# A two-block transformer layer on one core: the gate matrix made by adding scatter DMAs, and a reordered scan stage

## The reference

```python
def _gla_chunked(q, k, v, logf, s0):            # 8 heads, chunks of 64, two directions
    bc = cumsum(logf, axis=3)
    scores = where(incl, (q * exp(bc - ref)) @ (k * exp(ref - bc)).T, 0)
    o_intra = scores @ v
    def step(S, xs):
        o_c = (q * exp(bc)) @ S
        S = tot_c[..., :, None] * S + (k * exp(bc[-1] - bc)).T @ v
        return S, o_c
...
def _peer(h, w_query, sub_keys, expert_u, expert_v):
    q = (t @ w_query).reshape(n_tok, 8, 2, 128)
    sc = einsum('thcd,hckd->thck', q, sub_keys)
    s1, i1 = top_k(sc[:, :, 0], 16); s2, i2 = top_k(sc[:, :, 1], 16)
    top_s, top_i = top_k(s1[..., :, None] + s2[..., None, :], 16)
    e1, e2 = i1[top_i // 16], i2[top_i % 16]
    experts, gates = e1 * 128 + e2, softmax(top_s)
    act = gelu(einsum('td,tkd->tk', t, expert_u[experts])) * gates
    y = einsum('tk,tkd->td', act, expert_v[experts])
```

## Time and profile before

| | us |
|---|---|
| median of the runs | 5435.87 |
| the profiled execution | 5440.96 |
| its span, first to last instruction | 5439.2 |
| TensorE busy | 4832.4 (89%) |
| VectorE busy | 3114.6 (57%) |
| ScalarE busy | 2083.3 (38%) |
| POOL busy | 65.8 (1%) |
| scan stage | 3223 to 3549 |
| peer stage | 3769 to 5439 |

### The profile page before, as it was taken

The page is one execution under the profiler, slowest core; times in us unless marked ns, Lnnn a source line. Parts: engine busy times, 40 slices in busy tenths (PEclk is TensorE's granted clock), DMA queues, the critical chain, the costliest instruction groups (busy, mean ns, idle before and its releaser), DMA issues. The chain is left out here.

```text
span 5439.2 us, 67843 instructions
## 1 busy us (share of the span) xinstructions
PE 4832.4 (89%) x24244; PEld 3935.6 (72%) x24244; DVE 3114.6 (57%) x5040; ACT 2083.3 (38%) x2398; POOL 65.8 (1%) x137
## 2 busy tenths in 40 slices
PE   8926799999999569999799975677999999899998
PEld 3923477877877458878699965533888888788887
DVE  0062388888888642233688856512887666344444
ACT  1000267767767301111455545411333444322222
POOL 1000100000000100000000000000000000000000
PEclk9557899999999779999799986688999999999999
DMA  8412599999999623244111011142333454666663
GB/s 345 147 39 91 203 355 367 371 364 367 369 365 368 248 112 109 106 137 141 55 34 36 28 40 47 37 157 102 124 127 127 173 200 170 221 196 191 197 192 120
DMA packets 256059, 976.23 MB, mean 179 GB/s; under 512 B 27060, under 2 KB 63492, under 8 KB 202212
## 3 DMA queue, kind: packets, MB, share of 16 engines
q1 hardware_dynamic: 248516, 923.74, 47.5%
q0 software_dynamic: 7392, 50.50, 2.3%
HBM read 799.87 MB, written 174.28 MB: 179 GB/s over the span
## 5 line engine op out<-in xcount | busy, mean ns | idle before, releaser
L84 PE MATMUL peer_bank<-peer_t_high,peer_high 128*128 128x512 f32 x2176 | 856.4, 394 | 49.4 <-DVE peer_low L2771 35.8
L86 PE MATMUL peer_bank<-peer_t_high,peer_low 128*128 128x512 f32 x2176 | 849.9, 391 | 0.0
L85 PE MATMUL peer_bank<-peer_t_low,peer_high 128*128 128x512 f32 x2176 | 848.2, 390 | 0.0
L2771 DVE TENSOR_TENSOR peer_low<-peer_raw,peer_high 128x1024 fp32r<-128x1024 f32 x272 | 332.6, 1224 | 622.0 <-ACT peer_high L3112 622.0
L1076 DVE TENSOR_TENSOR moe_low<-moe_raw,moe_high 128x2048 fp32r<-128x2048 f32 x256 | 574.6, 2286 | 55.9 <-ACT moe_high L984 53.0
L84 PEld LDWEIGHTS peer_bank<-peer_t_high,peer_high 128*128 128x128 f32 x2176 | 409.9, 188 | 133.1 <-issue 50.6
L984 ACT ACTIVATE moe_high<-moe_raw 128x2048 fp32r<-128x2048 f32 x256 | 478.3, 1906 | 3.7 <-PE moe_up_bank L894 2.0
L3112 ACT ACTIVATE peer_high<-peer_raw 128x1024 fp32r<-128x1024 f32 x272 | 287.0, 1056 | 486.2 <-PE peer_bank L86 481.0
L86 PEld LDWEIGHTS peer_bank<-peer_t_high,peer_low 128*128 128x128 f32 x2176 | 409.5, 188 | 87.0
L85 PEld LDWEIGHTS peer_bank<-peer_t_low,peer_high 128*128 128x128 f32 x2176 | 410.0, 188 | 83.5
L1081 DVE TENSOR_TENSOR moe_low<-moe_raw,moe_high 128x2048 fp32r<-128x2048 f32 x128 | 293.0, 2289 | 66.4 <-ACT moe_high L989 66.4
(11 more groups left out here) (535 smaller groups left out, 9170.1 us busy)
## 6 DMA issues: line engine op xcount, KB each, us to landing
moe_raw<-w_gate_up SPq DMA_DIRECT2D x256, 1024.0 KB, 6.8
moe_raw<-w_down SPq DMA_DIRECT2D x128, 1024.0 KB
peer_raw<-expert_u SPq DMA_DIRECT2D x128, 512.0 KB, 3.7
peer_raw<-expert_v SPq DMA_DIRECT2D x128, 512.0 KB, 3.5
hidden<-peer_gelu SPq DMA_DIRECT2D x128, 256.0 KB
gate_matrix<-peer_stage SPq DMA_DIRECT2D x8, 4096.0 KB, 12.3
peer_stage<-gate_matrix SPq DMA_DIRECT2D x32, 1024.0 KB, 7.6
peer_stage<-hidden SPq DMA_DIRECT2D x128, 256.0 KB, 3.4
```

The lines of the kernel that those rows point to most:

```text
L84: pe.matmul(out, wh, xh, start=start, stop=False)
L85: pe.matmul(out, wh, xl, start=False, stop=False)
L86: return pe.matmul(out, wl, xh, start=False, stop=stop)
L2771: v.tensor_tensor(low_part[:, slot], raw[:, slot], high[:, slot].bitcast(F32), ALU.subtract).then_inc(cut_low, 1)
```

## The change

In the peer stage the one-hot matrices, the transposes of `chosen`, the quads, their evictions and the stores of `stage` are gone. VectorE makes for each head the cell number of each choice, (second key x 128 + first key) x 512 + token, in the tile `cell` (two new steps, `pair` and `cell`), and the gates in the tile `gate`. POOL then issues, for each head, 16 x 4 indirect DMAs that each add 128 gates, one a token, to their cells of `gate_matrix` in DRAM. Two choices of one token in different heads may be the same cell, so each head waits until all scatters of the heads before it have landed. The matrix must be zero before: POOL clears it in the scan stage with 32 DMAs of 1 MB, and waits for them at that stage's end. The matrix is now laid out [second key][first key][token], and is loaded one m at a time (256 KB, rows of 2 KB). SP waits for all 512 scatters ahead of the loads of the second pass. The gates, hidden tiles and products have a buffer `early` of their own (which before holds the tokens), and the high and low parts of the gated tiles have `hh` and `hl`. The loops of the stage are written out. The first unit of the second pass takes the upper four banks first. The root of the mean is a logarithm and an exponential on ScalarE in place of scale, root and reciprocal.

In the scan stage the outputs, their square and the sum of head p move from period p + 1 to p, and a copy `oc` of the output is made for `norm`. ScalarE makes the logarithms ahead of the values' copies; VectorE makes the forward cumulative sums of p + 1 ahead of the backward states of p. TensorE makes the forward updates ahead of the backward transposes, leaves out the product of each direction's last chunk, and turns the values ahead of the backward updates.

`DENSE` is 512, `TD` is 4.

```diff
@@ scan_phase @@
+        oc = [s.sb(f"oc{n}", [P, SEQ]) for n in range(2)]
+        zeros = s.sb("zeros", [P, 4, DENSE])
...
+            for n in range(PEER_KEYS // 4):
+                pool.dma_start(d["gate_matrix"][4 * n:4 * n + 4].rearrange("m e t -> e m t"), zeros[:]).then_inc(gates_cleared, 16)
+            pool.wait_ge(gates_cleared, 16 * PEER_KEYS // 4)
...
@@ scalar @@
                     keys(p, 1)
-                if head(p - 1):
-                    square_out(p - 1)
                 if head(p + 1):
                     sigmoids(p + 1)
                 if head(p - 1):
                     gates(p - 1)
                 if head(p + 1):
-                    values(p + 1)
                     logs(p + 1)
                 if head(p - 1):
                     log_out(p - 1)
+                if head(p + 1):
+                    values(p + 1)
+                if head(p):
+                    square_out(p)
@@ tensor @@
                     turn_keys(p, 0)
                     scores(p, 0)
-                if head(p - 1):
-                    outputs(p - 1)
-                if head(p):
+                    updates(p, 0)
                     turn_keys(p, 1)
-                    updates(p, 0)
                     scores(p, 1)
-                    updates(p, 1)
-                if head(p - 1):
-                    sums(p - 1)
                 if head(p + 1):
                     turn_values(p + 1)
+                if head(p):
+                    updates(p, 1)
+                    outputs(p)
+                    sums(p)
@@ vector @@
                     lengths(p + 1)
+                    sums_of_logs(p + 1, 0)
                 if head(p):
                     states(p, 1)
                 if head(p + 1):
-                    sums_of_logs(p + 1)
+                    sums_of_logs(p + 1, 1)
@@ peer_phase, vector @@
+                V.mark("pair", h, v.scalar_tensor_tensor(pair[:], key2[:], float(PEER_KEYS), key1[:], ALU.mult, ALU.add))
+                V.after(v, "pair", h)
+                V.mark("cell", h, v.scalar_tensor_tensor(cell[:, :, head(h)], pair[:, 0:TD], float(DENSE),
+                                                         token[:, 0:TD].unsqueeze(2).to_broadcast([P, TD, TOPK]), ALU.mult, ALU.add))
...
-            def rows(i, g):
...
+                V.mark("gates", h, v.tensor_tensor(gate[:, :, head(h)], eg[:], esum[:].unsqueeze(2).to_broadcast([P, TT, TOPK]), ALU.mult))
...
@@ sync @@
+            def load_gated(m):
+                need(sp, gated, m - 3)
+                sp.dma_start(gates[:, m % 4], d["gate_matrix"][m]).then_inc(gates_l[m % 4], 16)
+                sp.wait_ge(hid_stored[m % 2], 16 * (m // 2 + 1))
+                sp.dma_start(hid[:, m % 4], d["hidden"][m]).then_inc(hid_l[m % 4], 16)
...
+            for k in range(LAST):
+                if k == VBASE:
+                    sp.wait_ge(scattered, 16 * HEADS * TOPK * TD)
+                    for m in range(4):
+                        load_gated(m)
+                load(k)
+                if k == 1:
+                    sp.dma_start(keys, d["keysT"]).then_inc(k_l, 16)
+                if 4 <= k < VBASE + 4 and not is_query(k - 4):
+                    store_u(k - 4)
+                if k >= VBASE + 4:
+                    load_gated(k - VBASE)
@@ gpsimd @@
+            def scatter(h, k, t):
+                at_cell = bass.IndirectOffsetOnAxis(ap=cell[:, t, h * TOPK + k:h * TOPK + k + 1], axis=0)
+                pool.indirect_dma_start(out=cells, out_offset=at_cell, in_=gate[:, t, h * TOPK + k:h * TOPK + k + 1], in_offset=None,
+                                        compute_op=ALU.add).then_inc(scattered, 16)
...
+            for h in range(HEADS):
+                V.after(pool, "gates", h)
+                need(pool, scattered, 16 * TOPK * TD * h)
+                for k in range(TOPK):
+                    for t in range(TD):
+                        scatter(h, k, t)
@@ tensor @@
-            def quad(i, g):
-                pe.wait_ge(rows_made, i * QUADS + (g + 1))
-                need(pe, gtaken, i * QUADS + (g - 3))
-                for q in range(4):
-                    last = pe.matmul(gbank[g % 4][:, q], first[:, g % 4, q], second[:, g % 4, q], start=True, stop=True)
-                last.then_inc(multiplied, 1)
@@ scalar @@
+            for k in range(VBASE):
+                if k == VBASE - 1:
+                    high_hidden(0)
+                    high_hidden(1)
+                take(k)
+                cut(k + 3)
...
-            act.wait_ge(dve, at["mean"])
-            act.activation(root, root, ACT.Sqrt).then_inc(rooted, 1)
+            act.wait_ge(summed, DC)
+            act.activation(root, bank[0][:], ACT.Ln, scale=1.0 / D, bias=eps[:]).then_inc(rooted, 1)
+            act.wait_ge(rooted, 1)
+            act.activation(root, root, ACT.Exp, scale=-0.5).then_inc(rooted, 1)
```

More of the change, by code:

```diff
@@ L3099, in _ @@
-            groups(0, first=True)
-            with pe.Fori(1, PEER_KEYS // VG - 1) as i:
-                groups(i)
-            groups(PEER_KEYS // VG - 1, last_round=True)
+            pe.wait_ge(made, 7)
+            for k in range(VBASE):
+                if k < LATER and k % 8 == 3:
+                    h = k // 8
+                    if h == 0:
+                        pe.wait_ge(k_l, 16)
+                    pe.wait_ge(taken, h * 8 + 2)
+                    V.after(pe, f"r{TT - 1}1", h - 1)
+                    for t, c in ((t, c) for c in range(2) for t in range(TT)):
+                        last = pe.matmul(score[c][:, t], qs[:, c, t * P:(t + 1) * P], keys[:, h * 2 + c], start=True, stop=True)
+                    T.mark("scores", h, last)
+                unit(k)
```

538 lines of the change are left out of this document (196 added, 342 removed).

## The result

The changed kernel takes 5581.78 us (median of four runs, 5578.18 to 5582.29) against 5436.56 for the kernel before beside it: a ratio of 1.0262, 95% interval 1.0247 to 1.0278. It is 145 us slower, where the forecast was 172 us faster. The profiled execution took 5578.18 us, a span of 5576.4.

What follows compares the result with a forecast made beforehand. TensorE was taken to bound the peer stage, a chain of waits the scan. Products 120.7, gap 15.7, scan 36, clearing -2 and end 2 sum to 172 us saved: 5269 profiled, 5264 against the median; range 5240 to 5440.

Steps and rivals of the forecast that it cites:

- the price of one scatter: Peer stage: each of 512 adding scatters was taken to cost POOL 1.32 us, from plain indirect DMAs.
- the 21 of cover: Peer stage: at 1.32 us each the scatters end 21 us before the second pass needs them.
- The bounds, 1.28 and 2.25: Peer stage: us per scatter, from the plain indirect DMA to everything POOL does for one done twice.
- The break-even, 1.36: Peer stage: most us a scatter may take and stay covered; each 0.1 above delays the second pass 51 us.
- the covered case: The forecast: scatters end before the second pass needs them and the scan stage gains; 172 us saved, chance 0.50.
- Rival 1: POOL too slow, second pass waits: 5336 us at 1.5 per scatter, 5592 at 2.0; chance 0.20 below 1.70, 0.12 above.
- the third rival: Peer stage: POOL moves only while VectorE is idle, so scatters end 296 us late: 5560 us, chance 0.03.
- rival 2: First pass: DMA queues too slow for four-byte additions, from 0.103 us per element; about 6600 us at 0.3; chance 0.06.
- the 120.7 + 15.7 of products and gap: Peer stage: 120.7 us saved by removing one-hot products and transposes, 15.7 by closing the gap before the second pass.
- the 8 us after the last states: End of scan stage: one half of the outputs is left in place of both, saving 8 us.
- the 28 for the rounds: Scan stage: seven head pitches shrink from 37.5 to 33.5 us, saving 28 us.
- Rival 4: Scatters covered, but the scan stage's round doesn't shrink, since ScalarE waits for the outputs: 5300 us, chance 0.06.

Runs made afterwards that it cites:

- half and half: Against the changed kernel, token tiles 0 and 1 by adding scatters (256), tiles 2 and 3 by one-hot products, stores in 1 MB pieces: 5327.63 us, ratio 0.9793.
- the first of these runs: The changed kernel with its 512 scatters writing instead of adding: 5691.71 us, a ratio of 1.0474.

## Why the prediction was wrong

**The step that failed** is the price of one scatter: "I take 1.32, nearest to the only rows with indices". An addition takes 1.56 us of POOL in place of 0.97, so 1.86 us bare with the gap of 0.30, and 1.99 on average ((1033 - 16.5) / 511, without the draining, which the sum held apart): 0.67 more, and 512 times. That is 343 us; less the 21 of cover and the 7.5 by which draining was cheaper it is 314, and TensorE waited 310.6. The bounds, 1.28 and 2.25, held it. The choice between them did not: the rows it was nearest to had indices but no addition, and the addition was the part that no row showed. The break-even, 1.36, lay 0.08 above the lower bound and 0.89 below the upper. With a range placed like that the covered case should not have had 0.50 against 0.32 for POOL being too slow.

**The rule on the cost was right.** Rival 1 said that 2.0 us would give 5592; by the same rule 1.99 gives 5587, and it was 5582. The window was 721 us as worked out: gates of head 0 at 3804.1, SP at its wait at 4840.6 - 314.7 = 4525.9, 722 us later. From the release of SP to the first product of the second pass it took 4857.3 - 4840.6 = 17 us; the sum had 20 (4583.4 - 4563.6). Draining between heads took 16.5 us (24 in the sum).

**VectorE beside POOL.** I read its influence from two issues of the earlier trace rows as 1.28 to 1.32 us. For the adding scatter the median stays at 1.56, and single ones take up to 3.7. The trace shows which. Up to 4560 us there are 36 of over 1.9 us among 369, and every one begins while VectorE runs an instruction that reads two tiles in SBUF (`low`, L2782, or the three such steps of `heads`, L2817, L2847 and L2851); it is longer than 1.56 by what is left of that instruction, less some 0.12 us. None of them begins with VectorE idle, or under a maximum, an index search or a reduction. Where `low` follows such a step without a gap, the scatter waits for both:

```profile
3870.00 1.41 DVE L2817 TENSOR_TENSOR peer_shared<-peer_top 128x256 f32<-128x256 f32 x4
3870.24 3.74 POOL L2964 DMA_INDIRECT gate_matrix<-peer_gate,peer_cell  x1 [0.30 <-issue]
3871.33 1.21 DVE L2782 TENSOR_TENSOR peer_low<-peer_raw,peer_high 128x1024 fp32r<-128x1024 f32 x1
```

That is 2.18 us more, and the two VectorE instructions end 2.30 us after the scatter began. A `low` that begins after the scatter did changes nothing, and `low` itself isn't slowed (1.22 us, at most 1.28). The rule of the Trainium skill that the third rival rested on ("SBUF — State Buffer", section "SBUF: two separate sides") fits these scatters: POOL stands still while the other engine holds the ports that they share. The rival itself, POOL moving only while VectorE is idle, is out: VectorE was busy 270 of 360 us while 172 scatters were issued, and in all the long ones added 40 us of the 343.

**The queues (rival 2) are out.** With the queue of the scatters alone at work, then among the heads together with the weight loads:

```profile
q0 software_dynamic: 20160, 0.08, 21.8%
```

```profile
q1 hardware_dynamic: 16703, 47.19, 37.9%
q0 software_dynamic: 24595, 0.10, 21.4%
```

21.8% of 16 queues over 270 us for 20160 packets is 0.047 us a packet, above the 0.030 taken. The sum counted elements, 4096 a queue; but some 143 packets go with each scatter of 128, so it is 4580 a queue and 215 us of queue time where the sum had 123. That is still half of what would bind. The weight loads landed a little later (median of expert_u 4.4 us, 3.7 in the earlier trace rows), and TensorE was full in all of the first pass. The Trainium skill says of accumulating DMAs ("DMA: Bandwidth & Descriptors", section "Rules for kernel authors") that nothing is held between read and write; no run here tests it, and the price of a packet doesn't speak against it.

**What held.** From the first to the last product of the peer stage TensorE took 1631.7 us before and 1495.7 with half of the scatters: 136.0 for the 120.7 + 15.7 of products and gap. Up to the first product of the second pass it is 134.0 of these, and the second pass itself is 2.1 shorter, which is what the sum gave to the clock. The end gave 2.1 for 2. The scan stage gave 33.8 where the sum had 36 for the new order and -2 for the clearing.

**What held by chance.** The scan's order alone gave 31.8 for 36. The mis-sized term is the 8 us after the last states, of which 1.2 came; the 28 for the rounds held since the first round shrank by more than the others fell short. (The parts of the new round add up to 29.5 to 33.6, not 29.6 to 33.2.) And the clearing cost nothing that shows: the stage took 292.6 us with it and 296.7 without. Of that difference, 3 us lie in the outputs of the last head, whose state products (L2457, L2446 in the run without the clearing) took 2.79 and 1.90 us with it and 3.52 each without. Why the granted clock differed there is open. Rival 4 (the scan doesn't shrink) is out.

**Range and chances.** The range ended at 5440, no change; the time lay 142 us above it, in the 0.12 that I gave to a scatter of over 1.70 us.

## What to carry to other kernels

Work that is moved to an idle engine is free only up to a deadline: work out the break-even price per instruction, and when it lies close above the nearest row and far below the upper bound, forecast from the upper half, above all if the new operation has a mode (here the addition) that no row shows. An indirect DMA is paid by the instruction and hardly by the index, so count instructions; and when the idle engine can't carry all of the work, let it carry what fits under the cover and leave the rest where it was: half and half was faster than either. A price taken from a stretch where the engine is alone is too low for one where it has neighbours (1.92 against 2.11 us here). And a total that comes out right doesn't show that its terms did: the scan's order and the clearing were each off by several us here, in opposite directions.

## What was not expected of the hardware

- An indirect DMA of 128 elements that adds takes 1.56 us of POOL, one that writes 0.97; with 8 elements the adding one still takes 1.33, and 512 bytes for each index in place of 4 change nothing.
- An adding scatter that begins under a VectorE instruction with two inputs in SBUF takes up to 3.74 us in place of 1.56; one that begins before it is not longer, and VectorE isn't slowed.
- Beside plain indirect DMAs that follow each other every 1.2 to 1.4 us TensorE stands idle between products with nothing to wait for that the profile shows: busy 0.21 to 0.63, with DMA shares of 0.04 to 0.24 in the rows shown. At 1.8 to 2.1 us (additions, or plain ones paced by a memset) TensorE is full. Between these, the mean spacing alone doesn't order the stretches: 0.92 at 1.42 us once VectorE had finished the heads, 0.75 at 1.64, and 0.50 over 143 plain scatters in 240 us (1.68, with pauses of POOL among them) in the first of these runs. How POOL's issuing comes to hold back other engines is open; the profile names no releaser for these gaps.
- A store of one 4 MB block in runs of 256 bytes, on the queue of the weight loads, went with a stop of TensorE of up to 7.8 us; cut into four stores of 1 MB, one after each unit, it went with none.
